# Key and Fourier weight loads ahead of convolution rows, low parts ahead of a convolution tile, norm rows turned one group later

## The reference

```
hl = modulate(rms_norm(xl, norm_mix[l]), sh1, sc1)
pl = hl @ w_in[l]                     # columns: q, k, v, Fourier, three Hyena parts, three gates
xl = xl + g1 * mix_tokens(pl, ...)    # attention, 2-D Fourier mix, Hyena convolution, gates, w_out
h2l = modulate(rms_norm(xl, norm_ffn[l]), sh2, sc2)
xl = xl + g2 * moe_ffn(h2l, ...)      # 16 experts, top 2
# short_conv of a Hyena part u:  u[-1] * w[0] + u * w[1] + u[+1] * w[2] + b
```

## Time and profile before

| | us |
|---|---|
| median of three runs | 2034.55 |
| lowest, highest | 2030.69, 2035.2 |
| the profiled execution's own time | 2031.2 |
| its span, first to last instruction | 2029.6 |

### The profile page before, as it was taken

The page is one execution under the profiler, slowest core; times in us unless marked ns, Lnnn a source line. Parts: engine busy times, 40 slices in busy tenths (PEclk is TensorE's granted clock), DMA queues, the critical chain, the costliest instruction groups (busy, mean ns, idle before and its releaser), DMA issues.

```text
span 2029.6 us, 25897 instructions
## 1 busy us (share of the span) xinstructions
PE 1971.3 (97%) x9422; PEld 1573.5 (78%) x9422; DVE 1717.0 (85%) x1731; ACT 1161.4 (57%) x1134; POOL 197.6 (10%) x254
## 2 busy tenths in 40 slices
PE   7999999999999999999999999999999999999997
PEld 2787558778888888888888577687888888888885
DVE  3775689898688999999999978777799999999997
ACT  2323613323357777777777345344477777777774
POOL 2000110111030000000000300000100000000001
PEclk9999999999999999999999999999999999999998
DMA  8766417667389999999999768286799999999995
GB/s 338 276 230 218 143 59 236 242 222 267 147 290 402 402 397 394 398 396 395 397 400 387 261 212 280 49 332 228 256 374 391 400 395 394 391 405 387 404 385 225
DMA packets 181491, 629.47 MB, mean 310 GB/s; under 512 B 13904, under 2 KB 16092, under 8 KB 174369
## 3 DMA queue, kind: packets, MB, share of 16 engines
q1 hardware_dynamic: 150648, 503.62, 65.8%
q0 software_dynamic: 27808, 119.98, 16.1%
q10 hardware_dynamic: 2952, 4.77, 0.6%
HBM read 597.13 MB, written 31.19 MB: 310 GB/s over the span
## 4 chain that ended last, share of the span: by engine, by line
PE 79%; DVE 11%; DMA 5%; ACT 2%; issue 1%; SPq 1%; ACTq 0%; POOL 0%; DVEq 0%
PE bank L2493 74%; DVE work L1669 4%; PE bank L2503 4%; DVE ring L1669 2%; DMA work<-hp_dram 2%; DMA ring<-in_w_in_dram 1%; DVE m_lo L1669 1%; PE bank L2769 1%; PE bank L2520 1%; DMA ring<-in_w_exp_down_dram 1%; DVE w_lo L1669 1%; DVE work L2049 1%; ACT work L1420 0%; DVE work L1753 0%; DVE mixed L1669 0%
## 5 line engine op out<-in xcount | busy, mean ns | idle before, releaser
L1669 DVE TENSOR_TENSOR w_lo<-ring,w_hi 128x2048 fp32r<-128x2048 f32 x384 | 873.3, 2288 | 88.0 <-ACT w_hi L1532 85.5
L1532 ACT ACTIVATE w_hi<-ring 128x2048 fp32r<-128x2048 f32 x384 | 738.2, 1922 | 237.0 <-PE bank L2493 232.0
L2493 PE MATMUL bank<-w_hi,xsT_hi 128*128 128x512 f32 x1024 | 399.8, 390 | 0.8 <-DVE w_lo L1669 0.6
L2493 PE MATMUL bank<-w_lo,xsT_hi 128*128 128x512 f32 x1024 | 398.6, 389 | 0.0
L2493 PE MATMUL bank<-w_hi,xsT_lo 128*128 128x512 f32 x1024 | 315.4, 389 | 0.0
L1252 ACT ACTIVATE m_hi<-ring 128x1024 fp32r<-128x1024 f32 (+1 forms) x128 | 129.6, 1031 | 275.1 <-PE bank L2493 202.8
L2493 PEld LDWEIGHTS bank<-w_hi,xsT_hi 128*128 128x128 f32 x1024 | 192.2, 188 | 44.8 <-issue 1.9
L2493 PEld LDWEIGHTS bank<-w_hi,xsT_lo 128*128 128x128 f32 x1024 | 192.2, 188 | 40.2
L2493 PEld LDWEIGHTS bank<-w_lo,xsT_hi 128*128 128x128 f32 x1024 | 192.3, 188 | 38.6
L1669 DVE TENSOR_TENSOR m_lo<-ring,m_hi 128x1024 fp32r<-128x1024 f32 (+1 forms) x128 | 148.8, 1188 | 64.4 <-ACT m_hi L1252 62.6
L2493 PE MATMUL bank<-w_hi,hexpT_hi 128*128 128x512 f32 x512 | 202.3, 395 | 0.9 <-DVE w_lo L1669 0.9
(11 more groups left out here) (304 smaller groups left out, 2644.3 us busy)
## 6 DMA issues: line engine op xcount, KB each, us to landing
ring<-in_w_exp_gate_dram SPq DMA_DIRECT2D x128, 1024.0 KB, 9.1
ring<-in_w_exp_up_dram SPq DMA_DIRECT2D x128, 1024.0 KB, 8.5
ring<-in_w_exp_down_dram SPq DMA_DIRECT2D x128, 1024.0 KB, 8.5
ring<-in_w_in_dram SPq DMA_DIRECT2D x44, 1024.0 KB, 7.1
work<-in_w_mod_dram POOLq DMA_DIRECT2D x40, 1024.0 KB, 5.4
ys_dram<-work POOLq DMA_DIRECT2D x32, 512.0 KB, 7.8
work<-hp_dram SPq DMA_DIRECT2D x54, 256.0 KB, 3.9
work<-mod_dram POOLq DMA_DIRECT2D x8, 1024.0 KB, 9.0
```

Source lines behind the costliest of these rows:

```text
L1532: nc.scalar.activation(w_hi[:, pos % N_SPLIT, :], raw(i), ACT.Copy).then_inc(hi_done, 1)
L1669: return nc.vector.tensor_tensor(o, a, b, op)
L2493: return nc.tensor.matmul(o, a, b, start=first, stop=last)
```

## The change

SP: in layer 0 the rows of part c = 1 for the context blocks go behind the kv load, and all rows of c = 2 behind the f load. In layer 1 the third set of convolution weights and the rows of c = 1 and c = 2 go behind the kv and f loads. DVE: in layer 1 all four low quarters of q and the context rows' low parts, and two quarters of kv, go ahead of the second block of c = 0, and all of kv's ahead of c = 1. PE: in layer 1 the fillers of x2 and kv are removed; in layer 0 hT0, hT1 and the logits move one group of products later (the jobs list follows through the new function `output_steps`).

```diff
+def output_steps(l):
+
+    return [("o", 0, 0), ("o", 0, 1), ("o", 0, 2), ("o", 1, 0), ("o", 1, 1), ("o", 1, 2), ("hT", 0), ("o", 0, 3), ("r", 0),
+            ("hT", 1), ("o", 1, 3), ("r", 1), ("hT", 2), ("r", 2), ("hT", 3), ("r", 3)]
...
-                        elif key[2] in ("q", "kv") and not late_rows(l):
-                            for s in seqs:
-                                conv_rows(l, ("q", "kv").index(key[2]) + 1, s)
-                        elif key[2] in ("q", "kv", "f") and late_rows(l):
-                            conv_rows(l, ("q", "kv", "f").index(key[2]), 0)
-                            if key[2] == "q":
-                                conv_weights(l, 2)
+                        elif not late_rows(l):
+                            for c, s in {"q": [(1, 0)], "kv": [(1, 1)], "f": [(2, s) for s in seqs]}.get(key[2], []):
+                                conv_rows(l, c, s)
+                        elif key[2] == "q":
+                            conv_rows(l, 0, 0)
+                        elif key[2] == "f":
+                            conv_weights(l, 2)
+                            for c in (1, 2):
+                                conv_rows(l, c, 0)
...
                     low = split_low(("in", l, "q"))
-                    for _ in range(2):
-                        next(conv)
-                        steps_of(low, 2)
+                    next(conv)
+                    for _ in low:
+                        pass
                     for tb in late_rows(l):
                         low_rows(l, tb)
                     low = split_low(("in", l, "kv"))
+                    steps_of(low, 2)
+                    next(conv)
+                    steps_of(low, 2)
                     conv = convolve(1)
                     for _ in range(2):
-                        steps_of(low, 2)
                         next(conv)
                     low = split_low(("in", l, "f"))
                     conv = convolve(2)
...
                         for q in range(4):
-                            if q == 0 and l and key[2] in ("x2", "kv"):
-                                banks.append(begin(*names[0]))
-                                keep_busy(banks[0], 4)
                             pe.wait_ge(split_lo, n0 + q + 1)
...
-                for k in range(nt + 2):
+                for step in output_steps(l)[len(first_halves):] if turned_gates(l) else ():
+                    if step[0] == "hT":
+                        turn_row(1, step[1], step[1], h2row[step[1]])
+                    elif step[0] == "r":
+                        logits(step[1])
+                    else:
+                        b = begin("o", l, *step[1:])
+                        for q in range(4):
+                            out_part(b, *step[1:], q)
+
+                for k in range(nt + 2) if not turned_gates(l) else ():
```

More of the change, by code:

```diff
@@ L195, in plan_jobs @@
             job("dve", "mT", l, tb, half)
[L196 to L200, removed]
+    for step in output_steps(l) if turned_gates(l) else ():
+        if step[0] == "hT":
+            for half in range(2):
+                job("act", "hT", l, 1, step[1], half)
+        elif step[0] == "r":
+            job("act", "r", l, step[1])
+        else:
+            job("dve", "o", l, *step[1:])
+    for k in range(len(T) + 2) if not turned_gates(l) else ():
+        if k < len(T):
             for n in range(2):
```

## The result

The changed kernel takes **1.0046** of the time of the kernel before, interval [1.0035, 1.0058]: a median of 2042.88 us over five runs against 2033.91 beside them, about 9 us slower where 11.0 were forecast. The profiled execution took 2039.52, of which 2037.9 is its span, 8.3 more than before. In the changed kernel line 2508 is the matmul that was 2493, 1682 DVE's tensor operation, 797 the row read and 831 the weight load.

A forecast was written before the change was run, and what follows sets the result against it. PE, busy 97% of the span, was taken to bound the kernel, with time won or lost only at its waits and slow clock. +10.2 - 2.4 + 3.2 = +11.0 on 2032.9 gave 2043.9 us, range 2034 to 2053.

The forecast's parts named there:

- SP's order in layer 0: Layer 0: c = 2 rows wait behind f's second half, PE waits 11.0 us inside kv, f starts later: +10.2 us.
- the block's rows are there at 153.55 + 9.09: Layer 0: first c = 2 block's rows land 9.09 us after f's second half is issued at 153.55, at 162.65.
- The pair in layer 1: Half issued at 1189.89 and its third row's landing, 9.09 us in all, taken as model for layer 0's rows.
- The same bytes lie ahead: Layer 0: reason for taking 7.59 us to landing, the c = 2 rows having the same bytes ahead as the measured pair.
- The stretch at lower clock: Layer 0, kv after its long wait: one stretch of PE at the lower clock, adding 1.7 us.
- The turned rows: Layer 0's second norm: moving hT0 behind a group of products removes PE's 2.48 us wait near 523, -2.4 us.
- Layer 1, +3.2: Layer 1: q runs without its wait, but late c = 1 rows delay f's first low part from 1231.38 to 1234.6.
- is DVE's: Layer 1: the chain from f's first low part through turned queries to the attention is DVE's and keeps its length.
- Early rows: Rival, chance 0.14: rows land like lone ones, 3.8 us after issue, in both layers; +3.4 us, 2036.3.
- More behind the half: Rival, chance 0.12: rows land 12.38 us after issue in both layers; +20.6 us, 2053.5.
- The weights decide: Rival, chance 0.08: only f's lateness holds PE, so f follows kv straight in both layers; -12.3 us, 2020.6.
- The 1.7 that the prediction set on this stretch: Layer 1, q after its 1.92 wait: 3.40 us at half speed does the work of 1.7, so costs 1.7.

The follow-up runs named there:

- run 1: The changed kernel with layer 0's queue on SP put back, DVE, layer 1 and turned rows staying changed: 0.9998 of the kernel before.
- Run 3: The kernel before with only the new order of the turned rows in layer 0's second norm: 0.9978 of the kernel before.
- Run 10: The changed kernel with 18 filler products on PE between kv and f in layer 1: 1.0050 of the kernel before.
- Run 9: Changed kernel: layer 0's c = 1 rows before kv, c = 2 split before f's halves; layer 1's c = 1 between them, DVE turning before c = 2: 0.9948.
- run 4: The changed kernel with all of layer 1's part undone (fillers, DVE's order, SP's order): 1.0021 of the kernel before.

## Why the prediction was right, point by point

The time came within 1.0 us of the forecast of 2043.9. Part of that is luck: the change cost 9.0 and not 11.0, and the kernel before ran 1.0 above the 2032.9 from which the forecast starts.

**SP's order in layer 0, +10.2: right in mechanism, some 2 us too large in one term.** kv's second half went at 131.14 (131.6 forecast), f's second half at 152.90 (153.55), rows right behind. The step that was off is "the block's rows are there at 153.55 + 9.09": the third row landed at 159.96, 7.06 behind the half. The pair in layer 1 that stood for it was in a busier stretch. The table of stretches, first of the kernel before from that half's issue to the third row's landing, then of the changed kernel from 152.90 (the columns are each engine's busy time, PEclk, DMA share, GB/s):

```profile
1189.89:1198.98 9.09, 9.09 (x42) 7.58 (x41) 6.78 (x6) 3.67 (x4) 0.00 (x0) 1.00 0.97 334
```

```profile
152.90:159.96 7.06, 2.84 (x24) 2.64 (x23) 0.00 (x0) 2.17 (x3) 0.00 (x0) 0.89 0.86 303
```

3.04 MB went through in the first (9.09 x 334), 2.14 in the second, of which the half and the three reads are 1.84 in both. "The same bytes lie ahead" was true of these four and not of the rest. That took PE's wait from 11.0 to 9.03 and kv's end from 179.5 to 177.3. The stretch at lower clock took 2.0 instead of 1.7, but it adds nothing to the loss, here as in the prediction's own sum: kv's end comes from the fourth low part (176.6 + 2.9 there). f then ran at full clock without a wait, as said. Sum by the trace 8.4; run 1's 9.8 has in it the 1.1 by which its layer 0 is shorter than before. The fit of the Trainium skill ("DMA: Bandwidth & Descriptors", "Anatomy of one DMA") gave an estimate of 6.2 us for these bytes; 7.06 lies between it and the pair, nearer to it. The Trainium skill's statement in the same section, that a semaphore wait is on the issuing sequencer, is what the queue shows: row reads that need nothing of q's products began at 153.40, right behind the half that does.

**The turned rows, -2.4: right.** The wait went, no other came, 2.3 to 2.7 in the trace. Run 3 is on the larger side, 4.5 by its runs and 3.4 in its trace.

**Layer 1, +3.2: the total right by luck, since errors cancel.** q without a stall, kv in 11.7, the third row 11.63 behind the half (11.42 forecast) and the wait of 9.47 (8.9) are as worked out. f's first low part came 3.9 later against the layer's start instead of 3.2. The step that failed is that the chain from there to the attention "is DVE's". DVE's part of it did keep its length: from that low part's start to the last turned key it is 14.56 before and after. But the attention came 4.8 later, since f's products, at half clock, now ended behind the turned keys. DVE's last turned key and PE's next transposes, first in the kernel before, then in the changed one, where no wait is left:

```profile
1245.65 0.29 DVE L1669 TENSOR_TENSOR work<-work 128x128 f32<-128x128 f32 x1
1246.00 1.42 PE L2503 MATMUL bank<-const,work 128*128 128x128 f32 x11 [0.59 <-DVE work L1669]
```

```profile
1254.81 0.29 DVE L1682 TENSOR_TENSOR work<-work 128x128 f32<-128x128 f32 x1
1255.41 1.47 PE L2518 MATMUL bank<-const,work 128*128 128x128 f32 x12
```

Run 10 gave 0.8 of it back by holding the clock. The other miss is the 1.5 that came back at 1347, where the kernel before waits for gate weights; the prediction's own sum left that wait out. So 4.8 less 1.5 is near 3.2 by chance.

**The rivals.** Early rows: the lone landings of 2.6 to 3.8 did not hold behind a half; 5.6 from issue to landing. (They were not all without a load in front: kv's two smaller halves went out at 137.84, 3.9 us ahead of the reads from 141.70.) More behind the half: not 12.4 but 8.4 even in layer 1. The weights decide: it fell at its own condition, c = 2 rows by about 151. Run 9 keeps that condition, with the first c = 2 rows landed at 147.6, and there its prize in layer 0 is real: f follows kv with no wait, and layer 0 is 4.6 shorter than before, where 4.2 was worked out. Layer 1 gains 2.0 instead of 5.7. So that -11 in all is near the -12.3 is no test of the rival; run 9 has another order on DVE too.

## What to carry to other kernels

A transfer with a slot wait does not only come late itself; everything behind it on the same queue inherits the wait. Before moving a load ahead of others, write down when its own wait ends, and put what is needed sooner in front, or between its halves. And when a wait at the head of a chain goes, look for the next member: here f's low part, then the keys, then ACT's order.

## What was not expected of the hardware

The clock fell inside the long waits (at 158.5 and 1237.1) and stayed at 0.50 for 10.2 us, into the work behind. It does not follow the length of the wait alone. Waits of 2.48 at 523.44 in the kernel before and of 1.46 and 1.45 in run 1 left it at full; behind the 2.49 of run 9 it was low for 6.8 us. Even the same wait differs from run to run: after the 1.92 inside q of layer 1 the kernel before ran 3.40 us at 0.52, and runs 3 and 4, with that wait at 1.92 and 1.94, stayed at 1.00. PE's timeline of run 4:

```profile
1219.30 0.50 PE L2504 MATMUL bank<-m_hi,hT_hi 128*128 128x512 f32 x1 [1.94 <-DVE m_lo L1680]
```

Those two runs also show that a slow stretch need not cost what it loses. With q at full clock PE came to kv earlier and waited there for DVE (0.50 and 0.90 in run 4), and the attention started no earlier against the layer's start than in the kernel before. The 1.7 that the prediction set on this stretch was not there to be won.

In every traced kernel with the turned rows moved the clock also fell near 1140, in layer 0's end, for 3.4 or 6.8 us (1148.3 in the changed kernel), and in the one trace of the kernel before it did not, though PE's two waits there, 1.3 and 1.45, are the same. In the changed kernel that cost 1.7, most of which a later wait took up. Whether the moved rows cause it stays open.
